# POOL issues an expert's gathers ahead of another expert's add, in each pass of the expert loop

## What is computed

```python
scores = sigmoid(x2d @ router_w)              # (T, 64)
# the best 8 experts of each token, from the best 4 of 8 groups; gates normalised, times 2.5
def block_fn(args):
    t_idx, g, e = args
    xb = x2d[t_idx]
    hb = silu(xb @ exp_gate[e]) * (xb @ exp_up[e])
    return (hb @ exp_down[e]) * g[:, None]
routed = segment_sum(yb, buf_t, num_segments=T)
x = layer_norm(ALPHA * x + shared + routed)
```

## Time and profile before

| | |
|---|---|
| three runs | 1148.40, 1150.08, 1150.49 us, median 1150.08 us |
| the profiled execution | 1145.99 us, its span 1144.2 us |
| mean granted TensorE clock | 0.974 of full speed |
| busy: TensorE matmuls, weight loads | 1056.2 us (92%), 750.0 us (66%) |
| busy: VectorE, ACT, POOL | 710.3 us (62%), 243.6 us (21%), 361.6 us (32%) |
| moved by DMA | 282.43 MB, mean 247 GB/s |

### The profile page before, as it was taken

The page is one execution under the profiler, slowest core; times in us unless marked ns, Lnnn a source line. Parts: engine busy times, 40 slices in busy tenths (PEclk is TensorE's granted clock), DMA queues, the critical chain, the costliest instruction groups (busy, mean ns, idle before and its releaser), DMA issues.

```text
span 1144.2 us, 31366 instructions
## 1 busy us (share of the span) xinstructions
PE 1056.2 (92%) x13702; PEld 750.0 (66%) x13703; DVE 710.3 (62%) x1531; ACT 243.6 (21%) x503; POOL 361.6 (32%) x357
## 2 busy tenths in 40 slices
PE   8999997968899999999999999999999999999996
PEld 6877886756643576666666666666666666666662
DVE  0888969798675969645486554454544554454438
ACT  2156421337464120100110001100111001100113
POOL 2000010138000013344454444444444444434410
PEclk9998999979889999999999999999999999999998
DMA  7221141430464385799999999999999999999661
GB/s 215 74 56 50 43 97 39 87 107 6 162 207 148 136 322 224 277 368 361 359 374 357 372 367 352 367 349 360 355 360 359 354 350 358 361 364 353 169 179 76
DMA packets 91927, 282.43 MB, mean 247 GB/s; under 512 B 22494, under 2 KB 49631, under 8 KB 66949
## 3 DMA queue, kind: packets, MB, share of 16 engines
q1 hardware_dynamic: 74685, 243.55, 57.5%
q0 software_dynamic: 16160, 33.62, 11.9%
q10 hardware_dynamic: 944, 3.24, 0.8%
HBM read 260.93 MB, written 35.86 MB: 259 GB/s over the span
## 4 chain that ended last, share of the span: by engine, by line
PE 65%; DVE 8%; issue 4%; ACT 2%; DMA 1%; SPq 0%; DVEq 0%; POOLq 0%
PE ph L2395 32%; PE ph L2422 19%; PE ph L1555 3%; PE ph L1573 2%; DVE w_exp L176 1%; PE ph L1696 1%; PE pz_late L1596 1%; DMA w_exp<-scr_f 1%; PE pt L1488 1%; PE pst L1468 1%; DVE w_exp L2633 1%; DVE w_exp L2625 1%; PE pt L1482 1%; DMA scr_f<-arena,row 1%; PE pt L1491 0%
## 5 line engine op out<-in xcount | busy, mean ns | idle before, releaser
L2395 PEld LDWEIGHTS ph<-arena,w_exp 128*64 128x64 f32 x8192 | 353.8, 138 | 109.5 <-issue 107.8
L2395 PE MATMUL ph<-arena,w_exp 128*64 128x96 f32 x8192 | 390.1, 248 | 37.0 <-issue 31.1
L2422 PE MATMUL ph<-w_exp,arena 128*96 128x512 f32 x512 | 234.6, 602 | 0.0
L977 POOL DMA_INDIRECT x_area<-scr_x,piece_row x192 | 203.6, 1061 | 83.0 <-issue 56.7
L2457 POOL DMA_INDIRECT scr_f<-arena,row x62 | 91.5, 1475 | 272.1 <-PE ph L2395 237.8
L523 PE MATMUL pz<-w_exp 128*128 128x260 f32 x672 | 157.4, 392 | 0.3 <-ACT w_exp L335 0.3
L2422 PEld LDWEIGHTS ph<-w_exp,arena 128*96 128x96 f32 x512 | 78.4, 162 | 109.9 <-issue 103.2
L523 PEld LDWEIGHTS pz<-w_exp 128*128 128x128 f32 x672 | 128.9, 194 | 23.2 <-issue 2.7
L2440 DVE TENSOR_SCALAR arena<-ph,row_weight 96x512 f32<-96x512 f32 x64 | 47.8, 747 | 131.5 <-PE ph L2422 131.5
L2410 DVE TENSOR_TENSOR arena<-arena,ph 128x192 f32<-128x192 f32 x64 | 22.5, 352 | 169.9 <-ACT arena L2403 169.9
L2403 ACT ACTIVATE arena<-ph 128x192 f32<-128x192 f32 x64 | 21.1, 330 | 486.2 <-PE ph L2395 471.0
(11 more groups left out here) (387 smaller groups left out, 1042.1 us busy)
## 6 DMA issues: line engine op xcount, KB each, us to landing
w_exp<-in_exp_up_dram SPq DMA_DIRECT2D x64, 1024.0 KB, 10.8
w_exp<-in_exp_down_dram SPq DMA_DIRECT2D x64, 1024.0 KB
w_exp<-in_exp_gate_dram SPq DMA_DIRECT2D x64, 1024.0 KB
w_exp<-in_w_in_dram SPq DMA_DIRECT2D x22, 512.0 KB, 3.9
w_exp<-in_x_prompt_dram SPq DMA_DIRECT2D x8, 512.0 KB, 4.9
w_exp<-in_w_out_dram SPq DMA_DIRECT2D x2, 2048.0 KB, 11.0
w_exp<-scr_f SPq DMA_DIRECT2D x8, 512.0 KB, 7.5
x_area<-scr_x,piece_row POOLq DMA_INDIRECT x192
```

The source lines that it names most:

```text
L977: nc.gpsimd.indirect_dma_start(m.x_pieces[:, s, r, :], None, m.scr_x1.rearrange("t (q c) -> (t q) c", q=QUADS), bass.IndirectOffsetOnAxis( ...
L2395: last = nc.tensor.matmul(pgu[64 * half:64 * half + 64, s % 2, (2 * part + j) * CAP:(2 * part + j + 1) * CAP], w[job.slot][:, k, f0:P * ha ...
L2422: last = nc.tensor.matmul(pyl[0:CAP, c, :], hid[:, s % 2, j, :], m.expert_down[job.slot][:, j, c * 512:(c + 1) * 512], start=(j == 0), sto ...
```

## The change

In each pass of POOL's loop the gathers of expert q + 4 are issued first, and the add of expert q - 1 behind them. The waits go with their instructions: the gathers' wait for the list stands now ahead of the add.

```diff
         for q in range(E - AHEAD):
             pool.wait_ge(gu_done, q + 2)
+            gather(nc, m, pool, Job(q + AHEAD))
             if q > 0:
                 add_rows(pool, Job(q - 1))
-            gather(nc, m, pool, Job(q + AHEAD))
         for q in range(E - AHEAD - 1, LAST - 1):
             add_rows(pool, Job(q))
```

## The result

Four runs of the changed kernel took 1172.44, 1173.29, 1179.26 and 1179.85 us, median 1176.28 us. Four of the kernel before had a median of 1149.24 us. The ratio is 1.0236, with a 95% interval of 1.0212 to 1.0261: slower by 27 us. The range reached to 1172 us. The profiled execution of the changed kernel is the fastest of the four, 1172.44 us with a span of 1170.7 us; that of before took 1145.99 us. So 26.5 us have to be found between the two traces.

What follows compares the result with a forecast made beforehand. It took TensorE, busy 92% of the span and slowed in gate and up by POOL's issues, as the bound. Terms -6.8 + 16.2 = +9.4 us gave 1159.5 us on the median of 1150.08 us; range 1140 to 1172 us.

Steps and rivals of the forecast that it cites:

- TensorE resumes with the end of POOL's stretch: Gate and up matmuls: TensorE runs freely once POOL's issues end; basis for taking -0.15 us per ordinary pass.
- List passes: Passes whose gathers wait for a list: the add now follows the gathers and costs 1.16 us in each of 14, +16.2 us.
- The bound of 1.7 us a pass: Upper bound for a list pass's loss in gate and up: the add's 1.47 us and a little.
- Ordinary passes: The 45 passes whose gathers wait for no list: POOL's last issue ends 0.15 us sooner, -6.8 us in all.
- ordinary passes under 6.2 us: Gate and up matmuls of ordinary passes: a time under 6.2 us would show the forecast wrong and rival (b) right.
- one unbroken stop of a microsecond: Sign of being right: a list pass's gate matmuls take about 8.2 us with a single such stop.
- Later adds, sooner gathers: Adds issued 3.9 us later in ordinary, 6.6 us in list passes; VectorE's idle time covers it, sooner gathers gain nothing: 0.
- the tail: End of the loop: pass 59 ends in gathers and two adds, POOL done at the same time: 0.
- Rival (a): TensorE's breaks in gate and up have nothing to do with POOL; nothing moves, 1150 us; chance 0.17.
- Rival (b): Ordinary passes give back 0.4 us each, -18 us, list passes pay half, +8 us: 1140 us; chance 0.25.
- Rival (c): Adds land too late for the weighings, VectorE late beyond its idle 2.31 us: 1174 us; chance 0.08.
- The rule: Skill's statement that only VectorE and GpSimd wait on a shared port; by it the sum would be 0, not +9.4 us.

Runs made afterwards that it cites:

- the list passes alone: Kernel before, with gathers ahead of the add only in the 15 passes whose gathers wait for a list: 1177.68 us, ratio 1.0267.
- the fourth gather in its three forms: Kernel before plus an extra gather behind the third in 14 list passes: 128 rows, ratio 1.0187; nearly all out of bounds, 1.0157; 16 rows, 1.0279.
- the two kernels with held gathers: Order of before, third gather held until VectorE has turned a block, ratio 0.9626; the same with the second held too in list passes, 0.969.
- The held add: Changed kernel, with the add of list passes held until VectorE has turned the next block: 1160.16 us, ratio 1.0117.
- the ring: Changed order with every pass's third gather held until VectorE has turned a block, add behind it; waits close a circle: 1318.92 us, ratio 1.2195.

## Why the prediction was right or wrong

**Direction and mechanism: right.** The reading "POOL's issues slow the supply of TensorE's matmuls, and the end of a long stretch is paid in full" was made from a few passes of one trace. On chips that stop nine runs now bear it: the change three times, the list passes alone and the fourth gather in its three forms are all slower, by 1.4 to 2.9%, and the two kernels with held gathers are faster, by 3.7 and 3.1%. Its first part needs a narrower word: indirect DMAs, not issues. "TensorE resumes with the end of POOL's stretch" is not exact either: in list passes the last stop ends from 0.2 us before to 1.0 us behind the end of POOL's last indirect row, and 1.3 to 1.9 us behind its beginning.

**List passes, forecast 14 x 1.16 = +16.2 us: too small.** Measured +25.6 us. The nine passes in which the clock holds went from 6.85 to 8.13 us, +1.28 each, close to the 1.16 taken from the earlier trace rows; 14 x 1.28 is 17.9 us. The rest, 5 x (9.67 - 8.13) = 7.7 us, is the step that failed: I costed the stop at its own length and put what TensorE's clock does behind it at nothing, without a reason. The trace of before could not show it: its break of 1.05 us had no fall behind it. The bound of 1.7 us a pass held for the nine, not for the five.

**Ordinary passes, forecast 45 x -0.15 = -6.8 us: mostly absent.** The median pass gained 0.11 us, near the 0.15 expected, 5 us in all. But experts 12, 25 and 29, of the few that had their issues at another place before (the earlier trace rows for 25), went from 18.8 us together to 21.3, and the sum over 44 passes is -1.9 us. Of the 17 us between the forecast sum and the measured one, the list passes make 9.4 us, the ordinary passes 4.9 us, and terms that were not foreseen or are not of the change the rest. The sign "ordinary passes under 6.2 us" did not come: as the prediction counts, the median went from 6.52 to 6.42 us. The "one unbroken stop of a microsecond" came in some list passes, as in expert 46 (1.04 us); in others, as in expert 38, three or four short stops stand in its place.

**Later adds, sooner gathers, forecast 0: right for the change.** The landings ended ACT's wait in 49 passes, and VectorE's idle time before L2410 covered them. Expert 40 has 3.45 us of that idle time left in the pass whose weighing had waited for the landing. The held add (+1.2%) and the ring (+22%) show where the cover ends.

**The rest.** First four experts +0.7 us, not foreseen; the loop's start +2.4 us, not of the change; the tail 0, as said. The sum of the measured terms, 25.6 - 1.9 + 0.7 + 2.4 = 26.8 us, meets the 26.5 us within 0.3 us.

**Rival (a), the breaks have nothing to do with POOL**: false where there are breaks, by the fourth gather and the held one. **Rival (b), ordinary passes give back 0.4 us**: false; they give back 0.1. **Rival (c), landings too late**: false as the cause here. ACT's wait ended with a landing in 49 passes, but its condition (over 10.6 us from add to landing in a list pass, 11.2 us in an ordinary one) was hardly met: from the start of the add's row on POOL to the start of ACT's weighing it is 7.0 to 7.9 us for adds of list passes, and 7.4 to 11.4 us for the others, one of them over 11.2. The 11.8 us that the prediction took from the earlier trace rows as its worst case is longer than any of them.

**The rule weighed.** The rows showed TensorE stopping with POOL. The Trainium skill, SBUF — State Buffer, section "SBUF: two separate sides", says that TensorE never waits on anyone for its port. Runs and rule can both stand: POOL's arithmetic (1.31 us, at the same place) and a plain load stop nothing, and on two chips nothing stops at all. What the rule cannot do is to set the sum at 0, since TensorE loses time beside POOL's indirect DMAs all the same. That it waits for something other than a port is argued from the arithmetic, not shown.

## What to carry to other kernels

Read TensorE's idle time that ends with "issue" against the rows of the other engines before you call it noise: where it moves when POOL's indirect DMAs move, it is a cost that their order can change. Here two gathers beside the first 2.3 us of a row of short matmuls, and one alone at +5.31 us, were free; one more that followed the others without a rest was paid for. Cost a new stop by its length and by the clock behind it, from a pass that has both. And before you hold an instruction to get it out of the way, follow what is queued behind it: the same hold gained 3.7% with the add ahead of it (nothing on chips without stops), and the kernel lost 22% on one of those with the add behind.

## What the runs showed of the hardware

**Two kinds of chip.** The same kernel took 1142 to 1147 us on three chips and 1081 to 1082 us on two. On the first kind the gate and up of an expert take 5.26 us with POOL quiet and mostly 6.1 to 6.9 us beside its gathers; on the second 5.26 us always. The difference is in that group of matmuls, 411.1 us in the sum over the experts before against 336.4 us there in kernels whose time is within 0.3% of before (the kernel before itself has no trace there). That is 75 us, more than the 65 us between the times: their loop began 1 to 8 us later, and the rest of it took 242 to 251 us instead of 240. No row shows what makes the chips different, and as each chip had one batch, a chip and the state it was in can't be told apart.

**Where the stops come.** But for pauses of under 0.1 us they begin 2.2 us or more behind the first gate matmul, in most passes after 46 to 62 of the 128; where POOL's stretch began later, they began later too (after 97 in the earlier trace rows). They repeat every 0.7 us or so (pieces begin at 859.15, 859.88, 860.61 and 861.34 above). In list passes they end 1.3 to 1.9 us behind the beginning of POOL's last indirect row, whether that row takes 0.92 or 1.47 us. Between two stops of one row TensorE mostly gets one to seven matmuls.

**What of an issue makes them.** A gather of 128 rows, one with its rows out of bounds and one of 16 rows take POOL 1.00, 0.99 and 0.92 us and lengthen the products by 1.1 to 1.3 us. A plain load (0.61 us) and arithmetic (1.31 us) don't. The Trainium skill, DMA: Bandwidth & Descriptors, section "Terms", says that on this path POOL's software writes the descriptors to rings in SBUF. If writing them were the cause, 16 rows should cost less than 128 and the plain load of 128 rows as much as the gather; neither is so here. The packets on the queue of POOL's DMAs (q0) say the same: 16160 before, 16832 with the fourth gather and with the plain load alike, 48 more for each of the 14, and 16608 with the gather of 16 rows, 32 more each. The same skill's page Runtime: NRT & Kernel Launch, section "Instruction fetch mechanics", calls the fetching of an engine's instructions mostly hidden. The trace agrees, and speaks against such a wait as the cause of the stops: in the changed kernel the windows 862 to 867 and 950 to 953.7 us, with the late stops of experts 38 and 46, have no packet on the two queues of kind "instruction", and of the 103 stops of over 0.2 us in experts 4 to 61, 93 have none under way. The stops still look like a supply that is used up and then comes in small lots, but no run measured the supply, so that name for it stays an argument. Why an indirect DMA at work slows it, and why only on some chips, stays open.

**The clock.** On the chips that stop, list passes with an indirect issue behind the third gather had 3.4 us at the lower level (1.2 GHz) in 3 to 8 of the 14, at 1.5 to 1.8 us each. The number differs between the three profiled executions of the change: 5, 4 and 8, beside losses of 2.4, 1.4 and 2.9%. At 1.7 us a fall, four more falls are 7 us, half of the 14 us between the second loss and the third; between the first and the second, 8.5 us apart, one fall explains little. On these chips it fell outside the list passes too, though rarely: once at expert 3 in three runs, once at expert 12 in the run with the held add.
